# Streaming-encoder trunk on one core: the attention of layer 1 in three rounds per pair of heads instead of four

## The reference, cut to what matters

```python
q, k, v = split(x @ w_in, 3)                 # 512 x 1024 each, 16 heads of 64
s = einsum('bihd,bjhd->bhij', q_c * 64**-0.5, k_c) + bias
p = softmax(where(valid, s, NEG_INF))
o = einsum('bhij,bjhd->bihd', p, v_c)
y = o @ w_out
```

## Time and profile before

| | us |
|---|---|
| median of 3 runs | 1164.81 |
| lowest, highest | 1164.49, 1164.92 |
| the profiled execution's own time | 1165.25 |
| its span | 1163.5 |
| TensorE (matmuls) busy | 1153.6 |
| VectorE busy | 706.3 |
| ScalarE busy | 527.2 |
| GpSimd busy | 405.2 |

### The profile page before, as it was taken

The page is one execution under the profiler, slowest core; times in us unless marked ns, Lnnn a source line. Parts: engine busy times, 40 slices in busy tenths (PEclk is TensorE's granted clock), DMA queues, the critical chain, the costliest instruction groups (busy, mean ns, idle before and its releaser), DMA issues.

```text
span 1163.5 us, 18918 instructions
## 1 busy us (share of the span) xinstructions
PE 1153.6 (99%) x6958; PEld 1019.6 (88%) x6958; DVE 706.3 (61%) x1183; ACT 527.2 (45%) x917; POOL 405.2 (35%) x240
## 2 busy tenths in 40 slices
PE   9999999999999999999999999999999999999997
PEld 7888888989999998888887777788999999998886
DVE  5070173789888873443505676757888888854436
ACT  4355253335555554232425666662455555553222
POOL 2539415141111115446245343451311111144441
PEclk9999999999999999999999999999999999999999
DMA  6533314242222334325032212141213333233221
GB/s 220 181 127 109 109 37 145 71 148 96 92 103 108 108 108 145 109 75 179 19 109 73 91 46 91 46 150 69 73 73 110 108 108 108 108 117 118 90 73 73
DMA packets 21976, 119.89 MB, mean 103 GB/s; under 512 B 2448, under 2 KB 6672, under 8 KB 8992
## 3 DMA queue, kind: packets, MB, share of 16 engines
q1 hardware_dynamic: 15440, 104.96, 25.6%
q10 hardware_dynamic: 6480, 14.17, 3.6%
HBM read 117.02 MB, written 5.24 MB: 105 GB/s over the span
## 4 chain that ended last, share of the span: by engine, by line
PE 98%; DVE 1%; issue 0%; ACT 0%; POOL 0%; DVEq 0%; POOLq 0%; ACTq 0%
PE bank L1662 29%; PE bank L1664 29%; PE bank L1663 29%; PE bank L2074 2%; PE bank L2059 2%; PE bank L1693 1%; PE bank L1745 1%; PE bank L2095 1%; PE bank L2094 1%; PE bank L1943 1%; PE bank L1936 0%; PE bank L1951 0%; PE bank L1883 0%; PE bank L1929 0%; PE bank L1889 0%
## 5 line engine op out<-in xcount | busy, mean ns | idle before, releaser
L976 POOL TENSOR_TENSOR s_w_lo<-s_raw,s_w_hi 128x1024 fp32r<-128x1024 f32 x104 | 256.9, 2480 | 308.3 <-ACT s_w_hi L501 308.3
L1662 PE MATMUL bank<-s_t_hi,s_w_hi 128*128 128x256 f32 (+1 forms) x832 | 265.3, 319 | 0.0
L1664 PE MATMUL bank<-s_t_hi,s_w_lo 128*128 128x256 f32 (+1 forms) x832 | 263.0, 316 | 0.0
L1663 PE MATMUL bank<-s_t_lo,s_w_hi 128*128 128x256 f32 (+1 forms) x832 | 262.7, 316 | 0.0
L501 ACT ACTIVATE s_w_hi<-s_raw 128x1024 fp32r<-128x1024 f32 x111 | 116.4, 1060 | 223.8 <-PE bank L1664 191.6
L1001 POOL TENSOR_TENSOR s_w_lo<-s_raw,s_w_hi 128x512 fp32r<-128x512 f32 x36 | 64.2, 1783 | 305.2 <-ACT s_w_hi L601 305.2
L1664 PEld LDWEIGHTS bank<-s_t_hi,s_w_lo 128*128 128x128 f32 x832 | 158.6, 191 | 10.5
L1663 PEld LDWEIGHTS bank<-s_t_lo,s_w_hi 128*128 128x128 f32 x832 | 158.8, 191 | 9.3
L1662 PEld LDWEIGHTS bank<-s_t_hi,s_w_hi 128*128 128x128 f32 x832 | 158.7, 191 | 9.3 <-issue 0.2
L1228 DVE TENSOR_TENSOR s_a_lo<-s_act_a,s_a_hi 128x512 fp32r<-128x512 f32 x44 | 84.7, 1937 | 108.8 <-ACT s_a_hi L569 108.6
L1662 PE MATMUL bank<-s_w_hi,s_a_hi 128*128 128x512 f32 x352 | 137.1, 390 | 0.0
(11 more groups left out here) (213 smaller groups left out, 2078.9 us busy)
## 6 DMA issues: line engine op xcount, KB each, us to landing
s_raw<-stream SPq DMA_DIRECT2D x97, 1024.0 KB, 4.8
s_ln_gb<-ln_gb ACTq DMA_DIRECT2D x4, 1024.0 KB, 6.4
bias_rows<-rel_bias ACTq DMA_DIRECT2D x1, 3072.0 KB, 12.8
s_h<-x ACTq DMA_DIRECT2D x1, 2048.0 KB, 12.6
s_r_b<-bias_rows ACTq DMA_DIRECT2D x16, 128.0 KB, 2.2
s_x_t<-x_t ACTq DMA_DIRECT2D x3, 512.0 KB, 9.6
out<-s_h SPq DMA_DIRECT2D x3, 512.0 KB, 2.6
s_x_t<-x_t ACTq DMA_DIRECT2D x2, 256.0 KB, 5.8
```

Source lines behind the costliest of these rows:

```text
L976: nc.gpsimd.tensor_tensor(lo, raw[:, place // 2 % RAWS, n % 2, :], hi.bitcast(F32), ALU.subtract).then_inc(lo_done, 2 if n == 1 else 1)
L1662: nc.tensor.matmul(out, l_hi, r_hi, start=start, stop=False, skip_group_check=skip)
L1663: nc.tensor.matmul(out, l_hi, r_lo, start=False, stop=False, skip_group_check=skip)
L1664: return nc.tensor.matmul(out, l_lo, r_hi, start=False, stop=stop, skip_group_check=skip)
```

## The change

Tiles 0 and 1 of a pair become one round with four units. Their scores share a bank: tile 0 in columns 0 to 127, tile 1 in columns 128 to 383; the turned weights share banks 4 and 5 in the same way. In that round the units are numbered by head (head 0 tile 0, head 0 tile 1, head 1 tile 0, head 1 tile 1), and an engine that reads such a bank waits until both tiles of the head are in it (`bank_end`, and the wait on `s_done`). There are 24 rounds, three a pair. `weights_v` of the pair before, `k_low`, the head sums and the first of the two `split_hi` move to the round of tile 2. The pieces of a pair are 6, 3 and 7 in its three rounds, and 7 run ahead of the first. In the round of pair 6, tile 3 (`HEADS_FROM`), ScalarE takes the exponents before `weights_high`, and VectorE divides before `weights_low`. Part 2 comes ahead of the turned weights in the round of pair 7, tiles 0 and 1, and part 3 and 4 behind them; parts 5 to 7 stay in the round of tile 3. Line numbers above and below are those of the kernel before.

```diff
...
         def unit(s):
 
-            return s // PAIR_UNITS, s % PAIR_UNITS // 2, s % 2
+            p, i = s // PAIR_UNITS, s % PAIR_UNITS
+            return (p, i % 2, i // 2) if i < 4 else (p, i // 2, i % 2)
+
+        def stat(s):
+
+            p, t, hd = unit(s)
+            at = PAIR_UNITS * p + 2 * t + hd
+            return slice(at, at + 1)
+
+        def bank_end(s):
+
+            return s // 2 * 2 + 2 if s % PAIR_UNITS < 4 else s + 1
+
+        ROUNDS = [(p, tiles) for p in range(RPA_PAIRS) for tiles in ((0, 1), (2,), (3,))]
+        PER_PAIR = 3
+        INVERSIONS = PER_PAIR * (RPA_PAIRS - 1) + 1
+        HEADS_FROM = PER_PAIR * (RPA_PAIRS - 1) - 1
+
+        def units_of(r):
+
+            p, tiles = ROUNDS[r]
+            return slice(PAIR_UNITS * p + 2 * tiles[0], PAIR_UNITS * p + 2 * tiles[-1] + 2)
+
+        def range_of(r):
+            return range(units_of(r).start, units_of(r).stop)
+
+        def score_columns(t):
+            return slice(P, 3 * P) if t == 1 else slice(0, (t + 1) * P)
+
+        def columns_of(s):
+            return score_columns(unit(s)[1])
 
         def weight_blocks(s):
...
             def exponents(s):
                 _, t, hd = unit(s)
-                act.wait_ge(s_biased, s + 1)
+                act.wait_ge(s_biased, bank_end(s))
...
-            FIRST_HIGH = UNITS // 2 - TILES - 1
             act.wait_ge(normed[1], TILES)
-            for step in range(UNITS // 2):
-                p, t = step // TILES, step % TILES
+            for r, (p, tiles) in enumerate(ROUNDS):
                 ahead = p + 1 < RPA_PAIRS
-                if ahead and t == 1:
-                    k_high(p + 1)
-                if step == FIRST_HIGH:
-                    pair_high(0)
-                if ahead and t == 3:
-                    q_high(p + 1)
-                if step == FIRST_HIGH:
-                    pair_high(1)
-                exponents_first = t == 1 or step in (FIRST_HIGH + 1, FIRST_HIGH + 3)
-                if step == FIRST_HIGH + 1:
-                    weights_high(2 * step - 2)
-                if exponents_first:
-                    exponents(2 * step)
-                    exponents(2 * step + 1)
-                if step >= 1:
-                    if step != FIRST_HIGH + 1:
-                        weights_high(2 * step - 2)
-                    weights_high(2 * step - 1)
-                if not exponents_first:
-                    exponents(2 * step)
-                    exponents(2 * step + 1)
-                if p >= 1 and t == 0 and ahead:
-                    load_bias(p + 1)
-                if 1 <= p and t == (1 if ahead else 2):
-                    head_half(2 * p - 2)
-                    head_half(2 * p - 1)
-                if ahead and t in (1, 3):
-                    split_hi(RPA_KQ + 2 * (p + 1) + t // 2 + RING)
-                if step == FIRST_HIGH + 1:
-                    pair_high(2)
-                    pair_high(3)
+                here, before = range_of(r), range_of(r - 1) if r else ()
+                if tiles[0] == 0:
+                    exponents(here[0])
+                    exponents(here[1])
+                    for s in before:
+                        weights_high(s)
+                    exponents(here[2])
+                    exponents(here[3])
+                    if p >= 1 and ahead:
+                        load_bias(p + 1)
+                    if r == HEADS_FROM + 1:
+                        pair_high(3)
+                elif tiles[0] == 2:
+                    if ahead:
+                        k_high(p + 1)
+                    exponents(here[0])
+                    exponents(here[1])
+                    for s in before:
+                        weights_high(s)
+                    if p >= 1:
+                        head_half(2 * p - 2)
+                        head_half(2 * p - 1)
+                    if ahead:
+                        split_hi(RPA_KQ + 2 * (p + 1) + RING)
+                else:
+                    if r == HEADS_FROM:
+                        pair_high(0)
+                    if ahead:
+                        q_high(p + 1)
+                    if r == HEADS_FROM:
+                        pair_high(1)
+                    if r >= HEADS_FROM:
+                        exponents(here[0])
+                        exponents(here[1])
+                    for s in before:
+                        weights_high(s)
+                    if r < HEADS_FROM:
+                        exponents(here[0])
+                        exponents(here[1])
+                    if r == HEADS_FROM:
+                        pair_high(2)
+                    if ahead:
+                        split_hi(RPA_KQ + 2 * (p + 1) + 1 + RING)
...
-                dve.wait_ge(s_done, s + 1)
-                blk = bank[2 + hd][:, 0:keys]
+                dve.wait_ge(s_done, s // PAIR_UNITS * PAIR_UNITS + 3 + hd if t < 2 else s + 1)
+                blk = bank[2 + hd][:, columns_of(s)]
...
                 _, t, hd = unit(s)
-                dve.wait_ge(p_hi, s + 1)
+                dve.wait_ge(p_hi, bank_end(s))
                 nc.vector.tensor_tensor(pt_lo[:, weight_blocks(s), :],
...
-            for step in range(UNITS // 2):
-                p, t = step // TILES, step % TILES
-                bias_and_max(2 * step)
-                bias_and_max(2 * step + 1)
-                if p + 1 < RPA_PAIRS and t == 3:
+            for r, (p, tiles) in enumerate(ROUNDS):
+                ahead = p + 1 < RPA_PAIRS
+                before = range_of(r - 1) if r else ()
+                for s in range_of(r):
+                    bias_and_max(s)
+                if ahead and tiles[0] == 2:
+                    k_low(p + 1)
+                if ahead and tiles[0] == 3:
                     q_low(p + 1)
-                if t == 1:
-                    divide(step)
-                if step >= 1:
-                    weights_low(2 * step - 2)
-                    weights_low(2 * step - 1)
-                if p == RPA_PAIRS - 1 and t == 3:
+                if ahead and (tiles[0] == 2 or r == HEADS_FROM):
+                    divide(r)
+                for s in before:
+                    weights_low(s)
+                if 1 <= p and tiles[0] == (2 if ahead else 3):
                     head_sum(2 * p - 2)
                     head_sum(2 * p - 1)
-                if p + 1 < RPA_PAIRS and t == 1:
-                    k_low(p + 1)
-                if 1 <= p < RPA_PAIRS - 1 and t == 2:
-                    head_sum(2 * p - 2)
-                    head_sum(2 * p - 1)
-                if t != 1:
-                    divide(step)
-            invert_sums(slice(UNITS - PAIR_UNITS, UNITS), UNITS // 2 - TILES + 1)
+                if ahead and tiles[0] != 2 and r != HEADS_FROM:
+                    divide(r)
...
-            def scores(s):
-                p, t, _ = unit(s)
...
                     pe.wait_ge(q_lo_done, p + 1)
-                if s >= 2:
-                    pe.wait_ge(exp_done, s)
+                if p + t >= 1 and t != 1:
+                    pe.wait_ge(exp_done, PAIR_UNITS * p + 2 * t)
...
                 else:
                     pe.wait_ge(exp_done, s + 1)
-                if s >= 2:
-                    pe.wait_ge(p_lo, s - 1)
+                if s >= 2 and t != 1:
+                    pe.wait_ge(p_lo, s - 2 if (t, hd) in ((2, 0), (0, 1)) else s - 1)
+                first = columns_of(s).start
                 for j in range(t + 1):
-                    at = j if hd == 0 else t - j
-                    last = nc.tensor.transpose(bank[4 + hd][:, at * P:(at + 1) * P], r_p[:, s % 4, j * P:(j + 1) * P], ident[:, :])
+                    at = first + P * (j if hd == 0 else t - j)
+                    last = nc.tensor.transpose(bank[4 + hd][:, at:at + P], r_p[:, s % 4, j * P:(j + 1) * P], ident[:, :])
...
-            PIECES = (5, 2, 5, 4)
-            LEAD = 4
-            LAST_PARTS = ((0, 1), (2,), (), (3, 4), (5, 6, 7))
-            FIRST_PARTS = UNITS // 2 - len(LAST_PARTS)
+            PIECES = {0: (0, 6), 2: (0, 3), 3: (0, 7)}
+            LEAD = 7
+            LAST_PARTS = {HEADS_FROM: ((), (0, 1)), HEADS_FROM + 1: ((2,), (3, 4)), HEADS_FROM + 3: ((), (5, 6, 7))}
+
+            def early_part(part):
+                k = part // 2
+                pe.wait_ge(lo_done, place_of(RPA_OUT + k) + 1)
+                rpa_out_ready(k)
+                if part == 0:
+                    pe.wait_ge(k_lo_done, RPA_PAIRS)
+                if part == 1:
+                    pe.wait_ge(q_lo_done, RPA_PAIRS)
+                out_part(RPA_OUT, KD, lambda k: t_hi[:, k, :], t_lo, 2, k, 0, (part % 2,))
+
...
-            for step in range(UNITS // 2):
-                p, t = step // TILES, step % TILES
-                scores(2 * step)
-                first = 1 if step == 2 else 0
-                for piece in pieces[done:done + first]:
+            for r, (p, tiles) in enumerate(ROUNDS):
+                for t in tiles:
+                    scores(p, t)
```

(42 more changed lines are left out.)

28 lines of the change are left out of this document (14 added, 14 removed).

## The result

| | before | after |
|---|---|---|
| median of 18 runs each, same chip | 1164.90 us | 1167.11 us |
| lowest to highest | 1164.49 to 1165.26 | 1165.59 to 1169.64 |
| the profiled execution's own time | 1165.25 us | 1169.64 us |
| its span | 1163.5 us | 1167.9 us |
| its mean granted clock | 0.999 | 0.994 |

The ratio is 1.0020 (95% interval 1.0014 to 1.0027): 2.2 us slower, at the bound of what I had called "within 0.2%". I had forecast 1165.4 in a range of 1162.0 to 1168.0. The second row says more than the median. The kernel before stays within 0.8 us; the changed one spreads over 4 us, and its time follows, in the main, the mean clock of each run. At 0.999 it took 1165.59 and 1165.67; at 0.998 from 1166.76 to 1167.55; at 0.997 twice 1166.95; at 0.996 from 1167.16 to 1168.5; at 0.994 it took 1169.64.

What follows compares the result with a forecast made beforehand. TensorE, busy in 99% of the span, was taken as the bound. -2.6 + 2.5 + 0.7 = +0.6 us on the profiled 1165.25 gave 1165.9, or 1165.4 for the median, in a range of 1162.0 to 1168.0.

Steps and rivals of the forecast that it cites:

- One visit fewer: Scores of tiles 0 and 1 in one visit: 0.37 us saved a pair, 2.6 us over seven pairs.
- Waits that the shared bank adds: Steady pairs: VectorE and ScalarE wait for both tiles; the run of pieces covers it, so it costs nothing.
- Rival (c): Steady rounds: softmax chain over 1.8 us longer than counted, so TensorE waits; +4.2 us, 1169.6 us; chance 0.05.
- (d): Merged scores: the second tile pays as if alone; +1.8 us, 1167.2 us; chance 0.13.
- Moved products ... All nothing: Moved k and q pieces, their copies, slab splits and loads in the new rounds: all cost nothing.
- The end, where one split decides: End stretch: late split of slab RPA_OUT + 2 holds GpSimd, part 0 at 4.9 us, pair 7 2.5 later.
- Rival (a): End stretch: GpSimd reaches o_lo as early as before, no new waits; sum -3.5 us, 1161.3 us; chance 0.17.
- my three waits: From pair 7 on: part 4 0.6 us, transposes of tile 2, head 1 0.3, last transposes 0.5; 14.0 against 13.3.
- The sum: Whole kernel: -2.6 for merged visits, +2.5 and +0.7 at the end, +0.6 us on the profiled execution's 1165.25.
- rival (b): End stretch: a slab's late hi part makes TensorE wait another 2.4 us for GpSimd; +3.0, 1167.8 us; chance 0.13.

Runs made afterwards that it cites:

- kernel 1: The changed kernel with ScalarE's slab split ahead of the turned weights in the round of tile 2: 1165.88 us, ratio 1.0009.
- kernel 4: The kernel before, four rounds a pair, with only the split of slab RPA_OUT + 2 moved behind the last piece: 1168.68 us, ratio 1.0037.
- the first kernel of 5: The changed kernel with one piece between the scores of tiles 0 and 1 in pairs 0 to 6: 1172.21 us, ratio 1.0059.
- kernel 3: The changed kernel with only GpSimd's order changed, o_lo of pair 2 ahead of the low part of slab RPA_OUT + 3: 1168.54 us, ratio 1.0025.
- kernel 2: The changed kernel with ScalarE's split earlier and GpSimd's low part of slab RPA_OUT + RING - 1 behind o_lo of pair 2: 1164.08 us, ratio 0.9993.
- the second of 5: kernel 2 with one piece between the scores of tiles 0 and 1 in pairs 0 to 6: 1167.44 us, ratio 1.0022.

## Why the prediction was right, and what it missed

**"One visit fewer", 0.37 a pair: right in sum, with wrong terms.** The steady pair is 0.42 shorter, and parting the visit again costs 0.37 in two kernels. But of my three terms only the entry's 0.09 came out. The scores save 0.16 for the 0.22 forecast, since the merged visit takes 0.89 and not 0.81; the transposes save nothing for the 0.05; and 0.18 comes from the pieces, where I had nothing: the slow first step behind transposes once less, and slightly shorter steps in longer runs. That the sum still fitted is partly luck. Six pairs saved 2.45 us in the trace.

**"Waits that the shared bank adds", nothing: right** in the steady pairs, which are all busy. Rival (c) falls, and (d) with it: the second tile does not pay as if alone.

**"Moved products ... All nothing": wrong in pair 0.** It takes 0.29 longer instead of 0.37 shorter. I had counted pair 0 like a steady one. But in its first round no transposes and products of a pair before stand beside the six pieces, and ScalarE loads its table first (1.28 us from 627.04). The chain of exponents, divisions and minima for four units is then longer than what covers it. Pair 1 starts at 640.68 for 638.53 before, and three further pieces done by then account for 9 x 0.23 = 2.07, so it is 0.08 late in all: this execution reached its first scores some 0.2 early. With the 2.45 saved in six pairs that makes 2.37 for the 2.6 forecast, and the end stretch begins at 745.97 and not at 745.7.

**"The end, where one split decides", +2.5: right in its chain and its size.** 4.69 for the 4.9; kernel 1 removes it by moving the one split, kernel 4 makes it in the old rounds. Rival (a) falls with it. From pair 7 on, the first kernel of 5 took 14.09 for the 14.0 forecast, but not by my three waits. There was none at part 4 (forecast 0.6), 0.2 at the transposes of tile 2 (0.3) and 0.7 at the last transposes (0.5). The rest is a wait of 0.6 that I had not seen at all, the scores of tile 2 for exponents. So the sum is good and its terms are not.

**What the sum lacked is the clock.** The sum was +0.6. The two runs that kept a clock of 0.999 took 1165.6, 0.7 above the kernel before: in sum, waits and savings come out as forecast. The median lies 1.5 above those runs and the slowest 4. In the profiled run, the granted clock is 1.00 until TensorE has stood still for most of its 3.1 us, and 0.50 for about 10 us after, though it works without a pause from 750.66 on. Ten microseconds at half clock would cost some 5 of a TensorE that waits for nothing. By my estimate about 1 of that lies over waits that it would have had anyway: 0.3 over the end of the standstill and 0.6 ahead of the scores of tile 2, where this trace has none. That leaves the 4. I had written down the wait, 4.9 less what TensorE does in the meantime, and priced it at its length. Kernels 3 and 4 and the first of 5 have the same wait and the same low clocks; kernel 2, the second of 5 and all later ones have neither: that the one brings the other is shown. Why it comes in some runs and not in others is not. The measured 1167.1 lies in my range, but its upper end of 1168.0 was drawn for rival (b) and not for this; that it covered the median is luck, and the slowest runs, up to 1169.64, lie outside.

**My own marker misled.** I had said that an end stretch above 22.5 us means rival (b), one more link on GpSimd. It is 24.1, and the median fell near the 1167.8 of (b), but the link isn't there: GpSimd is ahead of every later part while TensorE runs at half clock. A length can't tell a wait from a slow clock; the window's clock column can.

## What to carry to other kernels

When rounds are merged, follow each operation that moves to a later point through every engine to the operand that TensorE next waits for; here one split on ScalarE, moved behind one more copy and with fewer pieces after it, cost 2.5 us, as much as the merged visits of six pairs saved. Putting it and one low part back in the order brought 1164.1, which is not clear of the kernel before; with the repairs in the last round and in pair 0 the merging pays (1162.2 us). In a kernel whose TensorE is busy in 99% of the span, a standstill of two or three microseconds can have a second price, the slow stretch behind it, here up to 4 us for a standstill of 3. Look at the clock column of the windows and at the spread of the runs with their mean clocks before explaining a median.

## What the hardware showed that I had not expected

A single standstill of about 3 us, in a kernel that otherwise keeps full clock, was followed by 10 us at the 1.2 GHz level in the traces of the changed kernel and of kernel 3, by 3.4 us in that of the first kernel of 5, and by none in that of kernel 4. One of 1.9 us (kernel 1) was followed by some 3.4, beginning when TensorE had been at work again for almost 2 us (pace 0.23 at 755.86 to 756.09, half clock from about 757.4). With the same kernel and the same wait, the mean clock of a run came out anywhere from 0.994 to 0.999. And scores that follow scores of another query tile, into another region of the same bank, step like neighbours, 0.12 us; only the step after that is 0.17 for 0.11. The Trainium skill, TensorEngine Tiling (Array Packing), Key Properties, has it that changing the tiling mode drains TensorE, and not just changing the tile (there a part of the array, which is what the two heads' matmuls alternate between). The row agrees.
